# Two mixing stages of a layer joined into one, with the projections of the first dealt out in portions among the steps of the second

## The reference, cut to what matters

```python
def token_mix(h, w_in, ...):
    (qkv, z, b_raw, a_raw, q_n, kc, vc, ks, vs, kw, vw, g_raw) = split_cols(h @ w_in, IN_SIZES)
    y_gdn = gated_deltanet(qkv, z, b_raw, a_raw, ...)                 # 4 heads of 128
    y_nsa = native_sparse_attention(q_n, kc, vc, ks, vs, kw, vw, ...) # 8 heads of 64
    return jnp.concatenate([y_gdn, y_nsa], axis=-1) @ w_out
```

## Time and profile before

| what | value |
|---|---|
| median of three runs | 4299.42 us (4298.81 to 4301.16) |
| profiled execution, time | 4298.11 us |
| profiled execution, span | 4296.3 us |
| PE busy | 4104.6 us (96%) |
| mean granted PE clock | 0.919 |
| mixing stage of layer 0, from its first projection to the norm after it | 641.3 us, granted clock 0.76 |
| the same of layer 1 | 638.5 us, granted clock 0.76 |

### The profile page before, as it was taken

One profiled execution on the slowest core, in us unless ns is written; L12 is line 12 of the kernel. 1 busy time (PEld: TensorE's weight loads), 2 busy tenths in 40 slices (PEclk: granted clock), 3 DMA queues, 4 the chain that ended last, 5 costly groups with the idle time before them and its releaser, 6 DMA issues.

```text
span 4296.3 us, 50018 instructions
## 1 busy us (share of the span) xinstructions
PE 4104.6 (96%) x20184; PEld 3393.1 (79%) x20184; DVE 1711.2 (40%) x3127; ACT 1378.1 (32%) x1848; POOL 1355.4 (32%) x298
## 2 busy tenths in 40 slices
PE   7999999999999999999979999999999997999998
PEld 7887887887888788888966788878888896667887
DVE  4777245534885444545434321011103543432110
ACT  4556224433222322233212232232223321223222
POOL 2223432222435444532000034444453201003445
PEclk9999999999999999989965699999998996569999
DMA  3111221111556555721200022332232111002233
GB/s 127 61 69 69 91 88 59 50 59 69 183 189 230 175 183 187 249 86 57 60 20 1 10 79 98 111 114 98 98 118 89 68 38 42 1 1 80 97 108 127
DMA packets 66353, 401.83 MB, mean 94 GB/s; under 512 B 7776, under 2 KB 8288, under 8 KB 27872
## 3 DMA queue, kind: packets, MB, share of 16 engines
q1 hardware_dynamic: 44624, 314.67, 20.7%
q10 hardware_dynamic: 21520, 84.16, 6.2%
HBM read 396.70 MB, written 2.10 MB: 93 GB/s over the span
## 4 chain that ended last, share of the span: by engine, by line
issue 76%; POOL 14%; PE 9%; POOLq 0%; DVE 0%; ACT 0%; DVEq 0%; ACTq 0%
POOL w_lo L331 14%; PE g L344 3%; PE g L345 3%; PE g L346 3%; PE p L405 0%; POOLq L327 0%; DVE x L1463 0%; PE p L429 0%; POOLq L330 0%; POOLq L331 0%; ACT L421 0%; ACT n_sq L413 0%; DVE h_lo L466 0%; DVE n_t L462 0%; ACT h_hi L443 0%
## 5 line engine op out<-in xcount | busy, mean ns | idle before, releaser
L331 POOL TENSOR_TENSOR w_lo<-w_raw,w_hi 128x2048 fp32r<-128x2048 f32 x294 | 1355.2, 4610 | 2930.6 <-ACT w_hi L338 2930.6
L344 PE MATMUL g<-h_hi,w_lo 128*128 128x512 f32 x2848 | 1135.3, 399 | 20.8 <-DVE h_lo L466 12.4
L346 PE MATMUL g<-h_hi,w_hi 128*128 128x512 f32 x2848 | 1115.7, 392 | 0.0
L345 PE MATMUL g<-h_lo,w_hi 128*128 128x512 f32 x2848 | 1114.4, 391 | 0.0
L338 ACT ACTIVATE w_hi<-w_raw 128x2048 fp32r<-128x2048 f32 x294 | 562.7, 1914 | 1191.1 <-PE g L346 1178.6
L344 PEld LDWEIGHTS g<-h_hi,w_lo 128*128 128x128 f32 x2848 | 539.1, 189 | 140.9 <-issue 21.3
L346 PEld LDWEIGHTS g<-h_hi,w_hi 128*128 128x128 f32 x2848 | 538.2, 189 | 114.9
L345 PEld LDWEIGHTS g<-h_lo,w_hi 128*128 128x128 f32 x2848 | 539.4, 189 | 112.8 <-issue 4.1
L344 PE MATMUL g<-act_hi,w_lo 128*128 128x512 f32 x880 | 352.3, 400 | 0.0
L346 PE MATMUL g<-act_hi,w_hi 128*128 128x512 f32 x880 | 347.8, 395 | 0.0
L345 PE MATMUL g<-act_lo,w_hi 128*128 128x512 f32 x880 | 347.8, 395 | 0.0
(11 more groups left out here) (389 smaller groups left out, 5215.4 us busy)
## 6 DMA issues: line engine op xcount, KB each, us to landing
w_raw<-in_stream SPq DMA_DIRECT2D x294, 1024.0 KB, 4.8
ada_w<-in_ada ACTq DMA_DIRECT2D x144, 512.0 KB, 4.6
n_w<-in_w ACTq DMA_DIRECT2D x8, 1024.0 KB, 14.1
x<-in_x SPq DMA_DIRECT2D x4, 512.0 KB, 6.5
out_x<-x SPq DMA_DIRECT2D x4, 512.0 KB, 2.6
masks<-in_masks SPq DMA_DIRECT2D x1, 1344.0 KB, 13.2
cols<-in_cols SPq DMA_DIRECT2D x1, 338.0 KB, 13.9
n_pos<-in_pos ACTq DMA_DIRECT2D x1, 256.0 KB, 6.6
```

The lines of the kernel that those rows point to most:

```text
L331: K.nc.gpsimd.tensor_tensor(K.w_lo[:, s], K.w_raw[:, s], K.w_hi[:, s].bitcast(F32), ALU.subtract).then_inc(K.sem("w_lo"), 1)
L344: nc.tensor.matmul(out, w_lo, h_hi, start=start, stop=False)
L345: nc.tensor.matmul(out, w_hi, h_lo, start=False, stop=False)
L346: return nc.tensor.matmul(out, w_hi, h_hi, start=False, stop=stop)
```

## The change

`gdn` and `nsa` become one stage, `mix`. The stream of weights is reordered: the four units of sparse attention come before the eight of the delta rule. After values, gates and the sparse attention's own units, the 16 tiles (12 of qkv, 4 of z) of the delta rule's projections are cut into 128 points of three matmuls (one k of one tile) and dealt out by the table `mix_points`: 48 points among the parts of the compression, 48 in the core (two a block in the first 16 steps, one in the others), and 8 each in four places after it. They use banks g0 and g1. The core has the one pair g2, g3 for scores: DVE writes scores and maxima to `n_p` in SBUF, so that the pair is free again after the maxima, and a block passes through the core in three steps in place of two. The first tap of the convolution is ACT's (`Identity` with a scale), the other three stay with DVE. The sums of squares of all eight heads stand together after the core, the heads alternate between p and g banks, and z waits as it is and gets its silu during the inverse. The output y goes to `h_hi`, `h_lo`, the place of the stage's input, sparse attention's half first. Buffers are laid out anew.

```diff
+def mix_points():
+    steps = [("lead", 8)] + [(("hid", 0, i), 2) for i in range(4)] + [("key", 4)]
+    steps += [(("hid", 1, i), 2) for i in range(4)] + [("val", 4), ("cmp", 6), ("prob", 4), ("turn", 6)]
+    steps += [(("core", t), 2 if t < 16 else 1) for t in range(32)] + [(("z", n), 8) for n in range(4)]
...
+    def feed(name):
+        for j in points.get(name, ()):
+            h, k = j // KD, j % KD
+            s, n = h // 2 % 2, h % 2
+            if k == 0:
+                if n == 0:
+                    pe.wait_ge(K.sem("w_lo"), pos.next("w_lo"))
+                pe.wait_ge(K.sem(f"g_free{n}"), pos.next(f"g_free{n}"))
+            w = slice(k * 256 + n * P, k * 256 + n * P + P)
+            last = three_pass(K, K.g[n][:], K.w_hi[:, s, w], K.w_lo[:, s, w], K.h_hi[:, k], K.h_lo[:, k], k == 0, k == KD - 1)
+            if k == KD - 1:
+                last.then_inc(K.sem("part"), 1)
...
     def scores(v):
-        if v >= 2:
-            pe.wait_ge(K.sem("n_pe"), pos.value("n_seen") + 2)
+        if v:
+            pe.wait_ge(K.sem("row_max"), pos.next("row_max", 2))
         for i in range(2):
-            t.matmul(K.g[2 * (v % 2) + i][:, 0:w], ...
+            t.matmul(K.g[2 + i][:, 0:w], ...
...
-    for v in range(len(work)):
-        if v + 2 < len(work):
-            scores(v + 2)
-        if v + 1 < len(work):
-            turned(v + 1)
-        weighted(v)
+    for step in range(len(work) + 2):
+        if 1 <= step < len(work):
+            scores(step)
+        if 1 <= step <= len(work):
+            turned(step - 1)
+        feed(("core", step))
+        if step >= 2:
+            weighted(step - 2)
+    feed(("z", 0))
+    feed(("z", 1))
+    pe.wait_ge(K.sem("n_acc"), pos.next("n_acc", 2))
+    for m in range(8):
+        token_sums_of(m)
+    feed(("z", 2))
+    pe.wait_ge(K.sem("m_tok"), pos.next("m_tok"))
+    spread(0)
+    feed(("z", 3))
+    products(0)
+    for qb in range(NB):          # transposes of n_y into g0 to g3
...
+    for h in range(1, 4):
+        spread(h)
+        products(h)
...
+    # ACT: first tap of a finished tile, then the split of the unit after next
+            act.activation(dst, K.g[h % 2][:], ACT.Identity, scale=K.col2("conv_w", h * 4 + 3), bias=K.col("zero")
+                           ).then_inc(K.sem("tap"), 1)
+            split_next(h)
...
+    # DVE, one step of the core
+        if 1 <= step < len(work):
+            maxima(step)
+        if 1 <= step <= len(work):
+            turned(step - 1)
+        convolved(("core", step))
+        if step >= 2:
+            added(step - 2)
```

More of the change, by code:

```diff
@@ new lines, in completed, with conv_then @@
+def completed(points, name):
+    return [j // KD for j in points.get(name, ()) if j % KD == KD - 1]
+def conv_then(K, pos, out, src, w, b, taps, sem):
+    v = K.nc.vector
+    v.tensor_scalar(out, src, w(taps - 1), b, ALU.mult, ALU.add).then_inc(pos.own, pos.tick())
+    pos.eng.wait_ge(pos.own, pos.ticks())
+    for d in range(1, taps):
+        step = v.scalar_tensor_tensor(out[:, d:], src[:, 0:T - d], w(taps - 1 - d), out[:, d:], ALU.mult, ALU.add)
+        if d < taps - 1:
+            step.then_inc(pos.own, pos.tick())
+            pos.eng.wait_ge(pos.own, pos.ticks())
+    step.then_inc(K.sem(sem), 1)
+    pos.eng.wait_ge(K.sem(sem), pos.next(sem))
@@ L1566, in pe_gdn @@
     gemm_tok(K, pos, 1, 32, at=256, free=False)
[L1568 to L1606, removed]
@@ L1631, in pe_gdn @@
+    swap(1)
     unit(2)
-    token_sums(1)
+    swap(2)
+    swap(3)
     unit(3)
-    token_sums(2)
-    unit(4)
-    token_sums(3)
-    half(5, 0)
+    swap(4)
+    feed("lead")
+    pe.wait_ge(K.sem("n_w1"), pos.next("n_w1", 64))
+    hidden(0)
+    swap(6)
+    swap(7)
+    pe.wait_ge(K.sem("n_hid"), pos.next("n_hid", 2))
+    for G in range(2):
+        last = t.matmul(K.p[2][64 * G:64 * G + 64, 0:31], K.col2("w2k", 0, 64), K.n_hid[:, G, 0, 0:31],
+                        start=True, stop=True)
@@ L2184, in act_nsa @@
                        ).then_inc(K.sem("n_tr0"), 1)
-        if v + 2 < len(work):
-            probs(v + 2)
-    pos.skip("n_o", 2)
+    taps("cmp")
+    probs(0)
+    for i in range(2):
+        act.wait_ge(K.sem("n_ct"), pos.next("n_ct"))
+        act.activation(K.n_pct[:, 4 * i:4 * i + 4].rearrange("p a b -> p (a b)"), K.p[i][:], ACT.Copy
+                       ).then_inc(K.sem("n_ctr"), 1)
+    taps("prob")
+    taps("turn")
+    for step in range(len(work) + 2):
+        if 1 <= step <= len(work):
+            turned(step - 1)
+        if 1 <= step < len(work):
+            probs(step)
+        taps(("core", step))
@@ L2313, in dve_nsa @@
     dve.wait_ge(K.sem("n_oc"), pos.next("n_oc", 4))
+    convolved("turn")
     def turned(u):
```

977 lines of the change are left out of this document (503 added, 474 removed).

## The result

| | time, us | against before |
|---|---|---|
| before | 4299.13 (4298.81 to 4301.16) | |
| after | 4110.61 (4105.93 to 4119.46) | 0.9563, 95% interval 0.9545 to 0.9581 |
| forecast | 4035, range 3975 to 4150 | |

Faster, as forecast, and inside the range, but 188.5 us were gained and not 264. The profiled execution of after took 4119.46 us, the slowest of its four, with a span of 4117.6.

The account below looks back on a forecast made before the run. PE, busy 96% of the span, was taken as the bound, at half clock in compression and core. Layer 0's six terms sum to 507.7 us against 641.3; 264.4 us saved over two layers gives 4035 us, range 3975 to 4150.

Parts of the forecast that it names:

- steps 1, 4, 5, 6: Layer 0's start, core to inverse, inverse and recurrence, tail: forecast at 80.9, 72.5, 86.1 and 63.2 us.
- step 4: From core to inverse: 72.5 us, bounds 68 to 80, with DVE setting the pace of heads 1 to 3.
- step 3: Core of 32 blocks with points: 133 us, steps of 3.0, 3.7, 4.05 and 5.1 us for 1 to 4 key blocks.
- its own conditions: Wrong if core clock is under 0.9, PE idles over 0.5 us a step there, or core to inverse exceeds 80 us.
- the term for POOL's port: In the core, DVE operations held up by three POOL splits of 4.6 us: 4 us a layer, bounds 0 and 14.
- step 2: Compression with 48 points: 72 us, bounds 58 with no wait and 134 if all stays at 1.2 GHz.
- The waits that I added up: In the compression, PE's waits for ACT's silu, the second blocking and the softmax: 3, 2 and 4 us, sum 9.
- The 5 us for the clock: In the compression, waits can drop the clock and points after them run at half: 5 us.
- A: Rival: queues cost each core step 1.5 us over PE's work, 112 us in all, kernel 4147 us; chance 0.22.
- B: Rival: clock stays at 1.2 GHz from the first hidden layer to the core's end, kernel 4360 us; chance 0.04.
- the core alone slow: Case: clock low in the core but not the compression, layer sum 617 us, kernel about 4254 us; chance 0.04.
- C: Rival: the core's last half, 3 and 4 key blocks, runs slow; 68 us a layer, kernel 4172 us; chance 0.04.

Follow-up runs that it names:

- e4_core_bare: Kernel after with the 48 points of projection moved from the core to the place ahead of it; 4215.82 us.
- e3: Kernel after without the maximum with 1e-30; the reciprocal is written to unused PSUM columns, and it and the gate product wait for the weighted sum; 4068.54 us.
- e9: Control of e3: same removal of the maximum and same wait for the weighted sum, but the reciprocal is written to SBUF; 4106.17 us.
- e10: e5 with DVE's order changed: both sines ahead of the convolutions, the second blocking ahead of the last one; 4040.38 us.
- e12: e10 with POOL's subtraction in four and, in each core step, DVE's convolution behind the additions; 4029.70 us, against 4029.37 without the convolution's move.
- e5: e3 with PE's swaps of tiles 6 and 7 ahead of hidden(0) and ACT's silu ahead of each hidden's last tap and split; 4071.97 us.
- e2: Kernel after without DVE's maximum with 1e-30 ahead of the reciprocal of the row sums; 4112.16 us.

## Why the prediction was right, and where it was not

Start, core to inverse, inverse and recurrence, tail (steps 1, 4, 5, 6): 80.5, 73.3, 85.6, 62.7 against 80.9, 72.5, 86.1, 63.2. The 3.53 us wait ahead of head 1 was there. But the heads did not go at DVE's pace, so step 4 came out near 72.5 partly by luck. A head took 7.11 us and not 7.8, PE was busy for 6.73 of it and DVE for 6.42, and DVE waited for PE between the heads. The operation put down at 1.47 us took 0.68. What that saved, about 2 us behind the wait, was spent ahead of it, where 44.0 us stand for 41.1.

The mechanism of the core (step 3) was right: thick matmuls (512 columns, the portions) among thin ones (64 rows or 64 columns, and transposes) bring the clock to 1.00, a step of n = 3 takes 4.26 us where it took 7.54 without points, and one pair of score banks costs nothing. e4_core_bare shows that it is the portions that bring it back soon after a fall. Steps at full clock took 2.78, 3.89, 4.26 and 5.36 us. By its own conditions, though, the prediction was wrong in the profiled layer 0: the clock in the core was 0.87, under 0.9, and PE idled 18.0 us in 32 steps, 0.56 a step and not 0.5 (in layer 1 0.94 and 0.56). The cause was named and too small: the term for POOL's port, 4 us with bounds of 0 and 14. Four splits fell into the core (POOL x4, 18.1 us) and not three, and the DVE stalls alone were 13.4 us, close to the upper bound. The rule of the Trainium skill on the shared port (page "SBUF — State Buffer", section "Who interferes with whom") pointed to that end of the bounds, and I should have gone by it. The stalls cost 28.5 us of core in layer 0, twice the bound, and 14.7 in layer 1, for the bound counted the operation that stands and not what the wait does to the clock. e3, e9 and the busy times show this.

Compression (step 2): 90.4 and not 72. The waits that I added up, 9 us, were 11.8. The 5 us for the clock were the mis-sized term: the second hidden layer ran its whole length at 0.50, with points between its parts, and of the 34 us at half clock in the stage PE was busy for about 32, which cost about 16. PE's work at full clock, put at 57.6, is then about 62.6: I halved all of the 48.9 us, though a mean clock of 0.55 says that a part of them was not at 0.50. With the waits gone (e10) the stage takes 68.1.

So the 76 us between forecast and measurement are the stalls with their half clock (42.1, after to e3), and the compression's queues with theirs (28.2, e3 to e10): 70.2 together. e10 has a stage of 509.2 and 509.5 us, where the sum said 507.7, and takes 4040 us, where it said 4035. Its parts are not that close: the core is 5.8 us over the sum, the start 1.6 over, the compression 3.9 under.

The rivals. A, a loss of 1.5 us a step by queues, comes near the measured time with two thirds of its 112 us, but not by its reason: apart from one wait of 1.88 us behind a convolution, steps without POOL's split are late by 0.54 us at most, and e12 gains nothing by another order. B and the core alone slow fell with the clock at 1.00. C too: the steps of n = 3 and 4 run at full clock except behind a stall, with transposes filling much of them. When the clock did fall, a step of n = 3 took 8.06 us, where C had reckoned 7.8.

## What to carry to other kernels

Where PE's clock hangs on a mix of thick and thin matmuls, price a wait by its length and then again by the steps behind it at half clock; here 12.5 us of waits came with 16.0 us of half clock in one layer and with 2.3 in the other, so the second part is a range and not a number. Before another engine's long operations are moved beside a chain of small ones, look at where the operands of the small ones lie: two columns written to PSUM instead of SBUF gave 38 us here. And when a wait is mended by moving work up in one queue, look at once for the next queue that the same consumer waits for: e5 gained nothing over e3, and e10, which is e5 with DVE's order changed too, 28 us.

## What was not expected of the hardware

- Of DVE operations of 128x2 in SBUF that started while POOL's subtraction ran, TENSOR_SCALAR (3.54, 3.92 us) and TENSOR_TENSOR (3.71) stood until it was through, and RECIPROCAL (0.17, and at most 0.168 over 128 records in e2 and e9) did not. With one operand in PSUM TENSOR_TENSOR took 0.16 beside it.
- PE at 0.50 for 125 us while busy without a break, in e4_core_bare, and at 1.00 for the 28.4 us behind it, on the same kinds of matmul.
- A fall of the clock with no wait ahead of it: at 1983.1 in e10, PE busy without a break for 43 us before, under 64 matmuls over 64 rows with 32 columns. In layer 1 the same at 3263.1.
- A wait of 1.88 us (before 2042.87 in after) was followed by the fall of the clock at 2044.7; in layer 1 of after the same wait (1.87 us, before 3366.21) was not. The one of 1.62 us at the same place was not in layer 0 of e3 (clock 1.00 to 2085), and was in its layer 1 and in e10 (0.50 from 2020.8). What decides between the two was not settled.
